# Neighbourhood bias blocks: one GpSimd addition for four heads in place of four VectorE instructions

## The reference

```python
# 4 blocks of 16 query columns, each with a band of 32 key columns and all 8 rows
bias = rpb[:, dr[:, None, None, :, None], dc[None, :, :, None, :]]
bias = jnp.where(col_ok[None, None, :, :, None, :], bias, -jnp.inf)
scale = HEAD_DIM ** -0.5                                   # 1/8
s_nb = jnp.einsum('bhrcqd,bhrwckd->bhrcqwk', qg, kg) * scale + bias
s_ctx = jnp.einsum('bhrcqd,bhjd->bhrcqj', qg, kc) * scale
p = jax.nn.softmax(jnp.concatenate([s_nb, s_ctx], axis=-1), axis=-1)
o = einsum(p_nb, vg) + einsum(p_ctx, vc)
```

## Time and profile before

| | us |
|---|---|
| median of three timed runs | 1978.0 (1976.04 to 1981.36) |
| profiled execution, its own time | 1975.02 |
| its span in the profile | 1973.2 |
| TensorE busy | 1730.3 (88%) |
| VectorE busy | 984.6 (50%) |
| ScalarE busy | 623.0 (32%) |
| GpSimd busy | 146.6 (7%) |

### The profile page before, as it was taken

How to read it: one execution, slowest core, us unless ns; L and a number is a source line. 1 busy time by engine, 2 the same in 40 slices (tenths; PEclk the granted TensorE clock), 3 DMA queues, 4 the chain that set the end, 5 groups by cost and what they waited for, 6 DMA issues and landing times.

```text
span 1973.2 us, 24651 instructions
## 1 busy us (share of the span) xinstructions
PE 1730.3 (88%) x10460; PEld 1525.4 (77%) x10460; DVE 984.6 (50%) x1606; ACT 623.0 (32%) x817; POOL 146.6 (7%) x184
## 2 busy tenths in 40 slices
PE   2799987857969999999999969998847899999996
PEld 1799955656959999999999959975535577887874
DVE  7844447782775554554622371116693343133334
ACT  3322235743252222221122152234543443232231
POOL 1000000000500000000000400001000300000003
PEclk9899998868989999999999989999858999999998
DMA  8443331001313333442422212242100223332332
GB/s 314 136 128 128 128 59 48 2 2 43 129 38 125 126 128 128 128 128 96 129 65 64 75 72 75 75 103 40 40 1 22 64 75 96 96 97 85 97 96 96
DMA packets 80238, 176.61 MB, mean 90 GB/s; under 512 B 38896, under 2 KB 39408, under 8 KB 79872
## 3 DMA queue, kind: packets, MB, share of 16 engines
q1 hardware_dynamic: 67008, 123.62, 20.5%
q0 software_dynamic: 13120, 51.41, 7.5%
HBM read 172.91 MB, written 2.10 MB: 89 GB/s over the span
## 4 chain that ended last, share of the span: by engine, by line
PE 78%; DVE 14%; ACT 4%; issue 2%; DMA 2%; DVEq 0%; ACTq 0%; SPq 0%
PE psum L692 69%; PE psum L798 2%; PE psum L754 2%; DVE s_sb L1147 1%; PE psum L809 1%; DMA ada_0a<-in_adaT 1%; DVE f_t L1101 1%; PE psum L832 1%; DVE hk L1269 1%; DVE x L1105 1%; DVE hd L1283 1%; DVE tmp L1079 1%; PE psum L722 1%; DVE psum L1345 1%; PE psum L949 1%
## 5 line engine op out<-in xcount | busy, mean ns | idle before, releaser
L692 PE MATMUL psum<-h_hi,w_hi 128*128 128x384 f32 (+1 forms) x1872 | 549.5, 353 | 56.5 <-DVE h_lo L1086 31.4
L692 PE MATMUL psum<-h_lo,w_hi 128*128 128x384 f32 (+1 forms) x1872 | 547.1, 352 | 0.0
L692 PE MATMUL psum<-h_hi,w_lo 128*128 128x384 f32 (+1 forms) x1872 | 546.4, 351 | 0.0
L1008 DVE TENSOR_TENSOR w_lo<-raw,w_hi 128x1024 fp32r<-128x1024 f32 x194 | 240.6, 1241 | 465.0 <-ACT w_hi L496 464.7
L692 PEld LDWEIGHTS psum<-h_hi,w_hi 128*128 128x128 f32 x1872 | 345.3, 190 | 81.0 <-issue 57.3
L496 ACT ACTIVATE w_hi<-raw 128x1024 fp32r<-128x1024 f32 x194 | 205.7, 1060 | 566.9 <-DMA raw<-in_wstream 566.9
L692 PEld LDWEIGHTS psum<-h_lo,w_hi 128*128 128x128 f32 x1872 | 346.3, 190 | 19.3
L692 PEld LDWEIGHTS psum<-h_hi,w_lo 128*128 128x128 f32 x1872 | 345.2, 190 | 19.9
L1019 DVE CUSTOM_DVE_ANT_0 psum<-ada_w,c_b 128x1024 f32<-128x1024 f32 x160 | 206.4, 1290 | 8.5 <-DVE ada_t L1019 0.2
L1047 DVE TENSOR_TENSOR tmp<-tmp,psum 128x768 f32<-128x768 f32 (+1 forms) x44 | 36.1, 821 | 279.9 <-PE psum L692 279.9
L692 PE MATMUL psum<-hid_hi,w_hi 128*128 128x384 f32 (+1 forms) x528 | 161.0, 359 | 15.4 <-DVE w_lo L1008 13.3
(11 more groups left out here) (168 smaller groups left out, 1525.4 us busy)
## 6 DMA issues: line engine op xcount, KB each, us to landing
raw<-in_wstream SPq DMA_DIRECT2D x196, 512.0 KB, 3.5
ada_w<-in_adaT POOLq DMA_DIRECT2D x80, 512.0 KB, 4.2
ada_0a<-in_adaT SPq DMA_DIRECT2D x6, 1024.0 KB, 14.4
fn_l<-in_dftL POOLq DMA_DIRECT2D x2, 2048.0 KB, 8.1
na_r<-in_rpb SPq DMA_DIRECT2D x64, 64.0 KB, 3.2
x<-in_xT POOLq DMA_DIRECT2D x2, 1536.0 KB, 14.2
ada_0b<-in_adaT SPq DMA_DIRECT2D x2, 1024.0 KB, 19.1
out_xT<-x SPq DMA_DIRECT2D x4, 512.0 KB, 2.8
```

The source lines that it names most:

```text
L692: mm = pe.matmul(ps[u][:, at:at + hi - lo], w[:, slot, k], r[:, k, lo:hi], start=first, stop=last)
L1008: dve.tensor_tensor(w_lo[:, k % RING].rearrange("p c n -> p (c n)"), raw[:, k % RING], w_hi[:, k % RING].rearrange("p c n -> p (c n)").bit ...
```

## The change

The bias block is made on GpSimd, by one addition of 128x1024 elements for the four heads, `na_b = na_r + na_m`, without the factor 8. For that, GpSimd's staging of the queries becomes a multiplication by 1/8, so that the scores of the latent blocks come out scaled; the exponential and the negated maximum of those units use 1.0 in place of 1/8. The context units keep 1/8. GpSimd makes each block's bias directly behind its staging. VectorE waits for `na_bias` at the places at which it made the block.

```diff
--- before.py
+++ after.py
@@ -307,6 +307,11 @@
         def local_keys(kind):
             return 384 if kind == "swa" else 256
 
+        def score_scale(kind, tile):
+
+
+            return 1.0 if kind == "na" and tile[0] else SCALE
+
         def key_count(kind, tile):
             return local_keys(kind) * tile[0] + CTX
 
@@ -460,13 +465,25 @@
                     link(ins)
                     for r in range(2):
                         q = u_t[:, QA + r, 0:LAT].rearrange("p (r c) -> p r c", c=GRID_W)
-                        ins = pool.tensor_copy(na_q[:, cb % 2, r].rearrange("p (r c) -> p r c", c=16),
-                                               backwards(q[:, :, 16 * cb:16 * cb + 16]))
+                        ins = pool.tensor_scalar(na_q[:, cb % 2, r].rearrange("p (r c) -> p r c", c=16),
+                                                 backwards(q[:, :, 16 * cb:16 * cb + 16]), SCALE, None, ALU.mult)
                     ins.then_inc(na_st, 1)
 
                 pool.wait_ge(mix_done, MIXERS * l + 1)
+                def band_bias(cb):
+
+                    if cb >= 2:
+                        pool.wait_ge(at_m, 2 * (unit0["na", l] + 2 * (cb - 1)))
+                    pool.wait_ge(na_ld[cb % 2], 16 * ROWS * (2 * l + cb // 2 + 1))
+                    v = na_b[:, 4 * (cb % 2):4 * (cb % 2) + 4].rearrange("p h (r c) -> p h r c", c=BAND)
+                    m = na_m[:, cb].unsqueeze(1).unsqueeze(1).to_broadcast([P, 4, ROWS, BAND])
+                    r = na_r[:, cb % 2].rearrange("p (r h c) -> p h r c", r=ROWS, h=4)
+                    pool.tensor_tensor(v, r, m, ALU.add).then_inc(na_bias, 1)
+
+                pool.wait_ge(na_mask, 16 * (l + 1))
                 for cb in range(4):
                     stage(cb)
+                    band_bias(cb)
 
                 pool.wait_ge(mix_done, MIXERS * l + 4)
                 tp, T = TP[l], width[l]
@@ -576,7 +593,8 @@
                             act.wait_ge(at_k, k0 + s - 2)
                         for j in range(2):
                             p = s_sb[:, s % 3, j, KEYS - n:last]
-                            act.activation(p, p, ACT.Exp, bias=nb[:, s % 3, j:j + 1], scale=SCALE,
+                            act.activation(p, p, ACT.Exp, bias=nb[:, s % 3, j:j + 1],
+                                           scale=score_scale(kind, tiles[s // 2]),
                                            accum_out=sums[:, s % 3, j:j + 1]).then_inc(at_p, 1)
 
 
@@ -1114,19 +1132,6 @@
                 U = 2 * len(tiles)
                 f0 = 0 if kind == "na" else 4
 
-                def band_bias(cb):
-
-                    if cb >= 2:
-                        dve.wait_ge(at_m, 2 * (u0 + 2 * (cb - 1)))
-                    dve.wait_ge(na_ld[cb % 2], 16 * ROWS * (2 * l + cb // 2 + 1))
-                    for h in range(4):
-                        v = na_b[:, 4 * (cb % 2) + h].rearrange("p (r c) -> p r c", c=BAND)
-                        m = na_m[:, cb].unsqueeze(1).to_broadcast([P, ROWS, BAND])
-                        r = na_r[:, cb % 2].rearrange("p (r h c) -> p r h c", r=ROWS, h=4)[:, :, h]
-                        ins = dve.scalar_tensor_tensor(v, r, 1.0 / SCALE, m, ALU.mult, ALU.add)
-                    ins.then_inc(na_bias, 1)
-                    dve.wait_ge(na_bias, 4 * l + cb + 1)
-
                 def score_max(s):
                     lat, i = tiles[s // 2]
                     n = key_count(kind, tiles[s // 2])
@@ -1148,7 +1153,8 @@
                                                  mx[:, s % 2, j:j + 1]).then_inc(at_m, 1)
                     dve.wait_ge(at_m, 2 * (u0 + s) + 2)
                     if kind == "na":
-                        dve.tensor_scalar(nb[:, s % 3], mx[:, s % 2], -SCALE, None, ALU.mult).then_inc(at_n, 1)
+                        dve.tensor_scalar(nb[:, s % 3], mx[:, s % 2], -score_scale(kind, tiles[s // 2]), None, ALU.mult)\
+                           .then_inc(at_n, 1)
                     else:
                         a = s % 2
                         dve.scalar_tensor_tensor(nb[:, s % 3], mx[:, s % 2], -SCALE, sinks[:, l, a:4 - a:3 - 2 * a],
@@ -1185,7 +1191,6 @@
                     dve.memset(na_b[:, 8], 0.0)
                     dve.wait_ge(nv_t, 5 * l + 1)
                     dve.tensor_copy(na_vc[:], ps_v).then_inc(nv_c, 1)
-                    dve.wait_ge(na_mask, 16 * (l + 1))
                 else:
                     dve.wait_ge(at_pre, l + 1)
                     dve.tensor_copy(sw_v[:].rearrange("p j d -> p (j d)"), ps[2][:, 0:TOK]).then_inc(at_pre_c, 1)
@@ -1204,7 +1209,7 @@
                     dve.wait_ge(at_ld, 16 * (l + 1))
                 for s in range(U + 3):
                     if kind == "na" and s % 2 == 0 and s // 2 < 4:
-                        band_bias(s // 2)
+                        dve.wait_ge(na_bias, 4 * l + s // 2 + 1)
                     if s < U:
                         score_max(s)
                     if kind == "na" and s % 2 == 1 and s // 2 < 4:
```

## The result

The changed kernel takes 1980.0 us (median of 17 runs, 1978.6 to 1981.6) where before takes 1976.2 us (17 runs beside them). The ratio is 1.0018 [1.0011, 1.0026]. Timed once more, it was 1.0024 [1.0015, 1.0033]. So it is slower by 3.6 to 4.7 us, about 0.2%, clear of no change in both timings, though the prediction had put the smallest measurable change at 0.3%. The forecast was 1985 us, +7.4 us on a kernel before of 1978.0; the time lies inside its range of 1976 to 1992, and the difference is half to two thirds of the forecast.

What follows compares the result with a forecast made beforehand. It took the kernel as a series of waits, TensorE holding 78% of the span. Code load 5.0 plus 1.2 us per attention layer (5.0 + 1.2 + 1.2) gave +7.4 us on 1978.0, so 1985.4 us; range 1976 to 1992.

Steps and rivals of the forecast that it cites:

- The load: Before layer 0's first query multiplication, GpSimd must load code with nothing to hide it: +5.0 us, once.
- Rival A: At GpSimd's code load in layer 0: already there, 37 ns are all; +2.4 us in sum, 1980.4 us; chance 0.22.
- The opening: Column block 0, layer 1: staging, addition, then first maximum in series, +0.4 us; by block 1 -0.6 us in all.
- The two engines block each other: Attention, both layers: normalisations 1 and 2 wait for whole GpSimd additions, 1.8 and 1.5 us in layer 1.
- Addition 1 is done well before it is needed: Block 1 of layer 1's attention: GpSimd's bias addition runs about 1352.7 to 1355.1 us, before the maximum at 1357.2.
- rival B: Both layers' attention: no code load and normalisations don't wait; -2.1 us, 1975.9 us, the most possible; chance 0.08.
- What is lost here arrives at the end in full: From the attention to the kernel's end: mixers run in series, no later slack swallows a loss or gain; no separate size.

## Why the prediction was wrong

- **The load** (5.0 us): wrong, and the step that failed. It was priced from how much could have been hidden behind the earlier trace rows and from ScalarE's table load, with no row of a load's length; the 37 ns that the trace had were right. The gap is 0.10 us, that of layer 1 without the instruction 0.09, and no cost of it can be put in (0.9997) or taken out (1.0032).
- **Rival A** ("the load is no load", 1980.4 us, no change that can be measured) is what came in its first half: there is no load. That its time meets the median to 0.4 us is luck. It stands on a kernel before of 1978.0 us, and the one measured beside the change took 1976.2; its sum of 2.4 us was too small for the timings (3.6 and 4.7) and more so for the phases, which grew by 6.8 us in the mean: +3.5 in layer 1 and +2.3 to +4.7 in layer 0.
- **The opening**: sized +0.4, measured +0.83 in layer 1. The query multiplication takes 1.04 us for two and not 0.53. It was forecast that by block 1 the maximum would be 0.6 us early; it came 1.99 us late. The air that this counted on was there and was won (1.02 us), but the negation's stop and TensorE's clock took it and more.
- **The two engines block each other**: the mechanism was right. It was placed on normalisations 1 and 2. Normalisation 2 is hit in both layers in each execution (2.68 us for 0.88). At block 1 the victim was another: the negation of the maxima, an instruction of 0.17 us whose new factor the prediction rightly took to cost nothing, and for which it did not ask what else runs beside it. It takes 1.3 or 2.1 us there. "Addition 1 is done well before it is needed" was true of its reader and left out the bystander. Normalisation 1 is not stopped in any of the three executions, since block 1 is later against the forecast than addition 2 is; in layer 0 it is normalisation 0, in one of three.
- **TensorE's clock** was in no term. A stopped VectorE leaves TensorE idle; the granted clock from 292 to 300 us falls from 0.86 and 0.79 to about 0.6, and the next scores and transposes take longer. In layer 1 these rows are 1.22 us longer at block 1. The runs with dead time on VectorE show the same without GpSimd: 2.3 us of delay became 3.0 of phase, and 5.0 became 6.7. No run holds the clock and keeps the stops, so the shares of layer 0 are not known.
- **The ceiling** (-2.1 us, rival B) was too high for the phase of layer 1, 1.36 us by its sum: it is 35.62 with VectorE's bias moved ahead of the signal and 35.63 with GpSimd's in four pieces, 0.45 us under before. Layer 0 can't be read so finely: 42.73 and 44.18 in two executions, where before has 43.18 and 44.01. The bias was cheap where it stood. The two timings, -3.8 and -1.6 us, do not rule out 2 us.
- **"What is lost here arrives at the end in full"**: held where a large loss made it visible (13.8 us in the phases, 13.4 timed). From the start of the first phase to the end, the change's three profiles are 5.3 us longer than before's two (1694.4 against 1689.1), and two timings say 3.6 and 4.7. The rest, 1 to 3 us between phases and timing, is not explained: executions of one kernel differ by 2 us in one stretch alone, and whether the changed kernel is luckier in it than the kernel before is open.

## What to carry over

Before work is given to GpSimd, look not only at when its reader needs it, but at every VectorE instruction from SBUF to SBUF that will arrive while it runs: here the multiplications by a number or a column were stopped (normalisation, negation), even one of two elements, until the GpSimd instruction was through; the reciprocal and what reads PSUM were not. If such work must go there, cut it: the stop was at most one piece here. Count what the stop does to the engine behind it too: TensorE, kept waiting, came back at a lower clock. And work on a busy engine is worth moving only as far as the other side of the wait lets it; here 1.35 us on VectorE were 0.1 us of time per block.

## What the hardware showed

- With MODIFY_POOL_CONFIG ahead of GpSimd's first multiplication the gap between two instructions is 0.10 us in two kernels; without it, it is 0.09.
- On GpSimd a multiplication of 128x128 with a constant takes 0.52 us at best, and two in a row 1.04; two copies of the same view take 0.53.
- VectorE's 128x2 negation (SBUF to SBUF) stands behind a GpSimd addition, up to 2.09 us for 0.17. Its reciprocal of the same 128x2 shape does not: it takes 0.147 to 0.167 us in all 40 cases of the changed kernel. It runs in the middle of an addition in the second execution of the kernel with additions 0 and 1 early; GpSimd's and VectorE's timeline:

```profile
292.95 2.36 POOL L480 TENSOR_TENSOR na_b<-na_r,na_m 128x1024 f32<-128x1024 f32 x1 [0.66 <-DMA na_r<-in_rpb]
...
294.13 0.17 DVE L1169 RECIPROCAL rinv<-sums 128x2 f32<-128x2 f32 x1 [0.92 <-ACT s_sb L599]
```

- The 16 first scores of layer 0 in the kernel before take 2.00 us in one execution, at a granted clock of 1.00 (2.4 GHz), and 3.68 in the next, at 0.54 on average, so nearly all at 1.2 GHz. TensorE's timeline in both:

```profile
285.40 2.00 PE L798 MATMUL psum<-u_t,na_q 64*128 64x256 f32 x16
```

```profile
286.62 3.68 PE L798 MATMUL psum<-u_t,na_q 64*128 64x256 f32 x16
```
